# Normalization and projection in one stage, with the first weight blocks multiplied tile by tile

## What is computed

```python
for l in range(DEPTH):                                     # DEPTH = 2
    mix = token_mixer_block(x, w_in[l], ...)               # h = x @ w_in[l], four mixers, ... @ w_out[l]
    x = layer_norm(ALPHA * x + mix, ln1_g[l], ln1_b[l])
    ffn = peer_ffn(x, peer_wq[l], peer_keys[l], ...)       # q = x @ peer_wq[l], top-16 of 16384 experts, ...
    x = layer_norm(ALPHA * x + ffn, ln2_g[l], ln2_b[l])

def layer_norm(x, g, b):
    mu = jnp.mean(xf, -1, keepdims=True)
    var = jnp.mean(jnp.square(xf - mu), -1, keepdims=True)
    return (xf - mu) * lax.rsqrt(var + LN_EPS) * g + b
```

## Time and profile before

| | us |
|---|---|
| median of 3 runs | 4332.21 (4329.56 to 4340.54) |
| profiled execution, its own time | 4323.45 |
| its span, first to last instruction | 4321.9 |
| PE busy | 3888.1 (90%) |
| DVE busy | 2806.0 (65%) |
| ACT busy | 1492.0 (35%) |
| POOL busy | 1321.6 (31%) |
| DMA | 838 MB, 194 GB/s over the span |

### The profile page before, as it was taken

How to read it: one execution, slowest core, us unless ns; L and a number is a source line. 1 busy time by engine, 2 the same in 40 slices (tenths; PEclk the granted TensorE clock), 3 DMA queues, 4 the chain that set the end, 5 groups by cost and what they waited for, 6 DMA issues and landing times. The chain is left out here.

```text
span 4321.9 us, 55240 instructions
## 1 busy us (share of the span) xinstructions
PE 3888.1 (90%) x19266; PEld 3386.4 (78%) x19266; DVE 2806.0 (65%) x5410; ACT 1492.0 (35%) x2146; POOL 1321.6 (31%) x1141
## 2 busy tenths in 40 slices
PE   7987899799889999999679878987997899999995
PEld 6865687589779999988568666875997889999884
DVE  3254434379987888877622644343799888888775
ACT  2232322234563333333222323222345633333331
POOL 0010000046674655532000100000566745555320
PEclk9997899899999999999889878998999999999997
DMA  4210222334369999999332103223443699999993
GB/s 152 82 56 1 95 95 97 122 128 162 132 230 348 353 361 338 346 331 331 139 118 78 56 1 102 95 90 122 142 169 133 225 352 356 354 344 334 340 331 119
DMA packets 263691, 838.45 MB, mean 194 GB/s; under 512 B 19553, under 2 KB 68705, under 8 KB 238433
## 3 DMA queue, kind: packets, MB, share of 16 engines
q1 hardware_dynamic: 189792, 567.92, 36.8%
q0 software_dynamic: 73728, 268.47, 16.8%
HBM read 749.81 MB, written 86.51 MB: 194 GB/s over the span
## 5 line engine op out<-in xcount | busy, mean ns | idle before, releaser
L845 POOL TENSOR_TENSOR ahead_u_low<-u_raw,ahead_u_high 128x1024 fp32r<-128x1024 f32 x96 | 256.8, 2688 | 1304.3 <-ACT ahead_u_high L840 1304.0
L86 PE MATMUL bank<-v_low,w_high 128*128 128x512 f32 x1536 | 597.7, 389 | 0.0
L87 PE MATMUL bank<-v_high,w_high 128*128 128x512 f32 x1536 | 597.6, 389 | 0.0
L88 PE MATMUL bank<-v_high,w_low 128*128 128x512 f32 x1536 | 597.6, 389 | 0.0
L890 POOL DMA_INDIRECT far_rows<-peer_v_dram,far_index x256 | 372.9, 1457 | 500.4 <-DVE x_far L914 456.1
L890 POOL DMA_INDIRECT far_rows<-peer_u_rows_dram,far_index x256 | 370.1, 1446 | 352.7 <-DVE far_dots L896 302.6
L1524 DVE TENSOR_TENSOR v_low<-v_raw,v_high 128x1024 fp32r<-128x1024 f32 x256 | 301.8, 1221 | 230.5 <-ACT v_high L1469 230.5
L1469 ACT ACTIVATE v_high<-v_raw 128x1024 fp32r<-128x1024 f32 x256 | 257.1, 1052 | 498.2 <-PE bank L88 498.2
L86 PE MATMUL bank<-xT_low,u_high 128*128 128x384 f32 x1088 | 370.8, 341 | 31.8 <-DVE u_low L1505 26.1
L87 PE MATMUL bank<-xT_high,u_high 128*128 128x384 f32 x1088 | 369.8, 340 | 0.0
L88 PE MATMUL bank<-xT_high,u_low 128*128 128x384 f32 x1088 | 369.8, 340 | 0.0
(11 more groups left out here) (337 smaller groups left out, 8365.4 us busy)
## 6 DMA issues: line engine op xcount, KB each, us to landing
u_raw<-peer_u_dram SPq DMA_DIRECT2D x128, 1024.0 KB, 7.3
v_raw<-peer_v_dram SPq DMA_DIRECT2D x128, 1024.0 KB, 7.6
gates_scratch<-stage SPq DMA_DIRECT2D x12, 4096.0 KB, 13.8
G<-gates_scratch SPq DMA_DIRECT2D x64, 768.0 KB, 7.3
in_raw<-w_in_dram SPq DMA_DIRECT2D x40, 1024.0 KB, 5.3
mg_raw<-w_merge_dram SPq DMA_DIRECT2D x52, 768.0 KB, 4.2
hidden_scratch<-ahead_hid SPq DMA_DIRECT2D x60, 384.0 KB, 2.5
hid<-hidden_scratch SPq DMA_DIRECT2D x30, 768.0 KB, 6.7
```

The lines of the kernel that those rows point to most:

```text
L86: nc.tensor.matmul(out, lh, rl, start=first, stop=False)
L87: nc.tensor.matmul(out, lh, rh, start=False, stop=False)
L88: return nc.tensor.matmul(out, ll, rh, start=False, stop=last)
L845: eng.tensor_tensor(self.ul[:, c], self.ur[:, c], as_f32(self.uh[:, c]), ALU.subtract).then_inc(self.u_low, 1)
```

## The change

Every normalization is put into one stage with the projection that reads its result.

- `enter_stage` takes the place of the opening stage (layer 0) and of `norm_stage("ln2")` plus `project_stage("in")` (layer 1). SP asks for the first weight block before the tokens. Two token-major blocks come first and are multiplied tile by tile: PE runs `first(t, 0)` (24 matmuls), transposes tile t+1, runs `first(t, 1)` (24 matmuls). VectorE, per tile: normalize, in tiles 0 and 1 split a weight block, split the tile, and copy out the bank of the tile before, which waits for `first(t - 1, 1)`. ScalarE splits weight block 0 before its first square root. Constants are made behind this. The input goes no longer through the output tensor; layer 1 keeps its residual in `x_res`.
- `query_stage` takes the place of `norm_stage("ln1")` and `project_stage("pq")`. The first two blocks of `peer_wq` are multiplied in two halves of the tokens: 8 x 24 matmuls of 256 columns for tiles 0 and 1, as many for tiles 2 and 3. The first half stands among the transposes. Two `clear` calls come ahead of it, where there were none ahead of `norm_stage` and one ahead of `project_stage`.
- `final_stage` normalizes and stores the last output, without transposes; it asks for the two parameter rows first. The full `clear()` stands before it, and none behind it.
- In `spread_stage` the store of hidden values is issued ahead of the gates' store, no longer behind it.
- The layers are a Python loop: no branch back and constant addresses. `u_raw` lies in `merged`, the norm's buffers in `projT`, `far_rows` and `keys`.

The diff, cut to its core (removed functions are those printed above):

```diff
+            def normalize(self, dve, link, t, add, before=lambda half: None):
...
+                    part = tok[:, half * 512:(half + 1) * 512]
+                    before(half)
+                    if add:
+                        link(V.scalar_tensor_tensor(out=part, in0=part, scalar=ALPHA, in1=bank[2 * t + half][:],
+                                                    op0=ALU.mult, op1=ALU.add))
+                    link(V.bn_stats(self.stats[:, t % 2, half, :], part))
+                link(V.bn_aggr(self.mv[:, t, :], self.stats[:, t % 2, :, :]))
+                V.tensor_scalar(self.std[:, t:t + 1], self.mv[:, t, 1:2], LN_EPS, None, ALU.add).then_inc(s["var_ready"], 1)
+                dve.wait_ge(s["std_ready"], t + 1)
+                link(V.reciprocal(self.rstd[:, t:t + 1], self.std[:, t:t + 1]))
+                link(V.tensor_scalar(rt, tok, self.mv[:, t, 0:1], self.rstd[:, t:t + 1], ALU.subtract, ALU.mult))
+                if t == 0:
+                    dve.wait_ge(s["rows_in"], 32)
+                link(V.tensor_tensor(rt, rt, self.g_row, ALU.mult))
+                V.tensor_tensor(tok, rt, self.b_row, ALU.add).then_inc(s["x_ready"], 1)
...
+                        def load(j, b):
+                            for r in range(2):
+                                if 2 * j + b:
+                                    sp.wait_ge(w_low, 4 * j + 2 * b + r - 1)
+                                sp.dma_start(raw[:, r], a["w_in"][layer, block_of(j, b)][:, 4 * r:4 * r + 4, :]).then_inc(loaded[r], 16)
+                        def store(t):
+                            if layer:
+                                sp.wait_ge(s["x_ready"], t + 1)
+                                sp.dma_start(a["x_res"][:, t], norm.tokens(t)).then_inc(s["x_out"], 16)
+                        if layer:
+                            sp.dma_start(norm.g_row, a["ln2_g"][layer - 1].partition_broadcast(P)).then_inc(s["rows_in"], 16)
+                            sp.dma_start(norm.b_row, a["ln2_b"][layer - 1].partition_broadcast(P)).then_inc(s["rows_in"], 16)
+                            load(0, 0)
+                            for t in range(1, NT):
...
                             for t in range(NT):
...
+                                sp.dma_start(norm.tokens(t), a["x"].rearrange("o (t p) d -> p (o t) d", p=P)[:, t]).then_inc(x_in[t], 16)
+                                if t == 0:
+                                    load(0, 0)
+                            sp.dma_start(lbl[:], a["hgrn_lb_logits"]).then_inc(once["lb_in"], 16)
+                        load(0, 1)
+                        store(0)
+                        store(1)
+                        sp.dma_start(w_ff[:], a["w_ff"][layer]).then_inc(small_in, 16)
+                        for r in range(2):
+                            sp.wait_ge(w_low, 3 + r)
+                            sp.dma_start(raw[:, r], a["w_in"][layer, 0][:, 4 * r:4 * r + 4, :]).then_inc(loaded[r], 16)
+                        store(2)
+                        store(3)
+                        for r in range(2):
+                            sp.wait_ge(w_low, 5 + r)
+                            sp.dma_start(raw[:, r], a["w_in"][layer, 1][:, 4 * r:4 * r + 4, :]).then_inc(loaded[r], 16)
...
+                        def first(t, b):
+                            tok = slice(t * P, (t + 1) * P)
...
+                                if k % 4 == 0:
+                                    pe.wait_ge(s["low_done"], 2 * t + (2 if b else k // 4 + 1))
+                                    pe.wait_ge(w_low, 2 * b + k // 4 + 1)
+                                mm = matmul_split(nc, bank[2 * t + b][:], (xh[:, k, tok], xl[:, k, tok]), (wh[:, b, k, :], wl[:, b, k, :]),
+                                                  k == 0, k == KT - 1)
...
+                        turn(0)
+                        for t in range(NT):
+                            first(t, 0)
+                            if t + 1 < NT:
+                                turn(t + 1)
+                            first(t, 1)
+                        with pe.Fori(1, n_T + 1) as j:
+                            pair(j, False)
+                        pair(n_pairs - 1, True)
...
+                    def keep_first(eng, copy, parity, t):
+                        eng.wait_ge(mm_done, 2 * t + parity + 1)
+                        copy(projN[:, parity, t, :], bank[2 * t + parity][:]).then_inc(kept[parity], 1)
...
+                        def high(j, b):
+                            if isinstance(j, int) and j == 1:
+                                act.wait_ge(mm_done, 7 + b)
+                            elif not isinstance(j, int) or j:
+                                act.wait_ge(mm_done, 8 * j + 4 * b - 4)
+                            for r in range(2):
+                                act.wait_ge(loaded[r], 32 * j + 16 * b + 16)
+                                nc.scalar.activation(wh[:, b, 4 * r:4 * r + 4, :], raw[:, r], ACT.Copy).then_inc(w_high, 1)
+                        high(0, 0)
+                        for t in range(NT):
+                            if layer:
+                                norm.root(act, t)
+                            if t == 1:
+                                high(0, 1)
+                            norm.high(act, t)
+                            if t:
+                                keep_first(act, copy, 0, t - 1)
+                        high(1, 0)
+                        keep_first(act, copy, 0, NT - 1)
...
+                        for t in range(NT):
+                            if layer:
+                                if t:
+                                    dve.wait_ge(x_in[t], 16)
+                                norm.normalize(dve, link, t, add=t > 0)
+                            if t < 2:
+                                low(0, t)
+                            norm.low(dve, t)
+                            if t:
+                                keep_first(dve, copy, 1, t - 1)
+                        low(1, 0)
+                        keep_first(dve, copy, 1, NT - 1)
+                        low(1, 1)
+                        if layer == 0:
...
+        def query_stage(layer, merged, early, keys, mixed, qT, load_next):
...
+                        def load(n):
+                            for r in range(2):
+                                if n == 0:
+                                    sp.wait_ge(wo_low, 6 + 2 * r)
+                                else:
+                                    sp.wait_ge(w_low, 2 * n + r - 1)
+                                sp.dma_start(wq_raw[:, r], a["peer_wq"][layer, n][:, 4 * r:4 * r + 4, :]).then_inc(loaded[r], 16)
+                        def store(t):
+                            sp.wait_ge(s["x_ready"], t + 1)
+                            sp.dma_start(a["x_mid"][:, t - 1], norm.tokens(t)).then_inc(s["x_out"], 16)
...
+                        store(1)
+                        load(1)
+                        store(2)
+                        store(3)
+                        load(2)
+                        load(3)
+                        sp.wait_ge(s["x_out"], 16 * DT)
...
+                        def half_tokens(n, part):
+                            b, cols, tok = n // 4, slice(n % 4 * P, (n % 4 + 1) * P), slice(part * 2 * P, (part + 1) * 2 * P)
+                            pe.wait_ge(s["low_done"], 4 * part + 4 if part else max(4, n + 1))
+                            for k in range(KT):
+                                if n % 4 == 0 and k % 4 == 0 and part == 0:
+                                    pe.wait_ge(w_low, 2 * b + k // 4 + 1)
+                                mm = matmul_split(nc, bank[n][:, tok], (wq_h[:, b, k, cols], wq_l[:, b, k, cols]),
+                                                  (xh[:, k, tok], xl[:, k, tok]), k == 0, k == KT - 1)
+                            if part:
+                                mm.then_inc(mm_done, 1)
+                        out_projection(0, 2)
+                        out_projection(2, 1)
+                        turn(0)
+                        out_projection(3, 1)
+                        turn(1)
+                        for n in range(3):
+                            half_tokens(n, 0)
+                        turn(2)
+                        for n in range(3, 6):
+                            half_tokens(n, 0)
+                        turn(3)
+                        for n in range(6, 8):
+                            half_tokens(n, 0)
+                        for n in range(8):
+                            half_tokens(n, 1)
+                        for n in range(8):
+                            b, cols = n // 4, slice(n % 4 * P, (n % 4 + 1) * P)
+                            pe.wait_ge(kept[n % 2], n // 2 + 1)
+                            for k in range(KT):
+                                if n % 4 == 0 and k % 4 == 0:
+                                    pe.wait_ge(w_low, 4 + 2 * b + k // 4 + 1)
```

(28 more changed lines are left out.)

715 lines of the change are left out of this document (341 added, 374 removed).

## The result

| | before | after |
|---|---|---|
| median of the runs, us | 4332.8 (4329.56 to 4340.54) | 4256.09 (4245.99 to 4258.57) |
| span of the profiled execution | 4321.9 | 4244.3 |

What follows compares the result with a forecast made beforehand. PE was busy 3888 of 4321.9 us, so only its other 434 us, or what is shortened at either end, could move the time. Gains 9 + 23 + 32 + 10 + 0 = 74 us off 4332.2 gave 4258, range 4236 to 4298.

Steps and rivals of the forecast that it cites:

- The opening: Start of layer 0: weights asked for early, first real matmul at 14.7 instead of 29.9 us; gain 9 us.
- the rest at nothing: Rest of the kernel: constant addresses and no branch counted in the other sums, other load and store orders unchanged; 0 predicted.
- Between the layers: Experts' end to layer 1's input projection: tiles alternate with matmuls; gain 23 us, bounds 15 to 28.
- Rival (2): Between the layers the clock stays low in the alternation, 192 matmuls at 0.42 us; 4286 us, chance 0.12.
- Out-projection and query: Out-projection and query stages, both layers: matmuls on token halves overlap normalization; gain 32 us.
- The step with the widest bounds: Query halves: a 256-column matmul costs 0.125 us, giving 32 us for two layers; 42 at 0.112, -8 at 0.177.
- Rival (1): Query halves: a 256-column matmul costs as much as a 384-column one, 20 us lost per layer; 4298 us, chance 0.08.
- (6): Query halves: weight load stands in full ahead of each 256-column matmul, 36 us more per layer; 4330 us, chance 0.01.
- Rival (3): Query halves: clock stays low there too, 34 us more per layer; 4354 us with low clock between layers, chance 0.04.
- The end: Final normalization stage: shorter tiles, last tile neither transposed nor split, earlier loads, small clear gone; gain 10 us.
- Spread to experts: Spread's end: hidden values' store issued first starts experts 8.3 us earlier, but a later wait takes it back; gain 0.
- rival (4): Spread to experts: the reordered store's 16 us for both layers come through; 4242 us, chance 0.10.

Runs made afterwards that it cites:

- experiment 8: Changed kernel, but at the opening SP asks for all four token tiles before the first weight block; 4259.1 us, ratio to before 0.9834.
- Experiments 6 and 11: Changed kernel with each 256-column query matmul split: into two of 128 columns (6), 4353.6 us; into 192 and 64 columns (11), 4435.0 us.
- experiments 1 and 2: 1: changed kernel with the old order of the two spread stores put back, 4256.6 us; 2: kernel before with only that order turned round, 4335.5 us.

## Why the prediction was right

- **The opening**: 9.2 for 9, in part by luck. The start held, at 14.49 for 14.7, with the halves landed at 7.10 and 9.60 for 7.1 and 9.7, and experiment 8 confirms the price per MB. But the two rows that were named for it, 8.2 us for 2 MB and 5.3 for 1 MB, give 2.9 us per MB and 2.4 of latency, and not 2.5 and 2.3: the number was right and its working was not. And a tile's transposes among the matmuls cost 0.79 us (21.99 to 22.78), since they ran at the full clock, and not 1.7: 2.4 in all for 5.1. What took this back stands below, under the rest at nothing.
- **Between the layers**: 22.0 for 23. The start was 2.9 us too early in the forecast. The halves landed 8.6 and 11.1 us behind the stage's start for 6.9 and 9.4, and I left out a table load of 1.28 us ahead of the first root. On this the Trainium skill ("ScalarE: Activation LUTs", "What ACT_TABLE_LOAD costs") has 1.283 us for the load, and this trace agrees (1.28); it adds a drain of 1.38 for each switch, which no row here shows, the root starting at 2111.60, 0.02 behind the load. The alternation went as told, and with less of the clock: low until 2124.5 and once more for 3.4 us, so the charge of 5 us was too high: the 192 matmuls ended 80.7 us behind the stage's start, 76.8 without any charge, with 2.9 of the difference from the late start. Rival (2) is out by PEclk 0.94 from 2120 to 2182.
- **Out-projection and query**: 43 for 32, the largest miss, in the right direction and of 11 us. Per layer, the first query matmul came 2 us earlier behind the merge's end than forecast (64.9 for 66.9; the two clears cost 1.9 and 2.1 for 2.4), and the rest took 99.4 us for 102.7: 384 x 0.0045 = 1.7 because 256 columns take 0.1205 and not 0.125, the other 1.6 because the transposes of tiles 2 and 3 with the wait for tile 3's split took 2.8 for 4.0 and the wait for block 1 took 2.1 for 2.6. The clock was priced rightly: two low stretches of 3.4 us, half of which is 3.4, for 3.3 (1.8 in the first banks and 1.5). The step with the widest bounds, -8 to 42, was decided by reading 256 columns off the line through 384 and 512. Experiments 6 and 11 show that this was right with little to spare: the line ends between 192 and 256 columns, at a floor of 0.111. Nothing on record had told where it ends, so that it held at 256 is luck in part. The bound from the 128-column row, 0.112, was the floor itself and no part of a line. Rival (1) is out, and so is (6): load and columns do not add up even at 64 columns.
- **Rival (3)**, the low clock in the halves, did not come, but my reason against it, that matmuls standing back to back run at 2.4 GHz, is refuted by experiments 6 and 11. It held at 256 columns and failed for 34 us at 128. A chance of 0.04 was too little for what was then known. Nor does the trace of before bear out what the prediction cites on transposes and the clock. The 0.50 of rows 3 stands over a stretch in which PE was idle for 21 of 29 us and so does not tell. At the opening PE did nothing but the 32 transposes from 8.99 on (rows 4), and the clock rose among them, at 12.57: the first sixteen starts stand 0.213 us apart, the last fourteen 0.109. Its window:

  ```profile
  12.60:14.40 1.80, 1.80 (x17) 1.57 (x15) 1.80 (x4) 1.73 (x4) 0.00 (x0) 1.00 1.02 410
  ```

- **The end**: 9.2 for 10, with the parameter rows landing ahead of the tokens and a tile's period of 7.01 for 6.93.
- **Spread to experts**: -2.3 for 0, and rival (4) is out by experiments 1 and 2. The reason given (u(1) is asked for only behind the gates' store) is right for half of it: with the request moved, 4 us of each layer's 8 come back, and the other half hangs on the gates' own load and the products behind it, which I had not named.
- **The rest at nothing**: the six channel-major blocks of the input projection, which the change only puts behind two token-major ones, got slower. Their matmuls stand 0.2333 us apart at the full clock, before 0.2289, in both layers: 576 x 0.0044 = 2.5 us a layer. In the opening this made good the transposes that had been priced too high, and between the layers it took back what the clock had left. The mixer and merge stages lost 1.4 and 1.7 us. It is hardly an accident: these two took 437.2 to 437.8 us in the two kernels with the loop (each layer on its own), and 438.7 to 441.7 in the twelve written out but for one layer of one, 436.9. About 1 us of it lies in a stretch with long idle times of PE (365 to 415 us before, 356 to 407 after), where the granted clock was 0.70 and is 0.67. Why stays open for both; no experiment was made on them.
- The sum was 74 of 77.6 us. The errors of +11, -3.1, -2.3 and four of 1 or less partly cancel, and inside the opening and the stretch between the layers larger ones do. The count of the chances had 0.94, 0.02 and 0.04 where the rivals' own add up to 0.95, 0.01 and 0.04.

## What to carry to other kernels

Between a normalization and its projection, it is the interleaving of tiles with multiplications that paid here, and an engine's order paid again: look for what stands in an in-order engine behind an operation that waits for a transfer, such as a root of 0.2 us behind a split. Cut matmuls for the sake of overlap only down to a width at which columns still set the time and the clock still comes up; here 256 columns gave 18 us over whole tokens, 128 lost 84, and 192 with 64 lost 166. And an empty stretch that a change only moves is still worth a look: clearing semaphores while others worked gave 18 us, a quarter of what the whole change had given. And compare the stages that a change leaves alone: a matmul slower by 0.0044 us cost 5 us here.

## What the runs showed of the hardware

- Matmuls that each load 128 columns of weights never stood closer than a floor, by the medians: 0.111 to 0.112 us for 64, 128 and 192 columns at 2.4 GHz, 0.213 at 1.2 GHz, there for 256 columns too. At 2.4 GHz 256 columns took 0.120, 384 took 0.173 to 0.178, and 512 took 0.227 (experts) to 0.234 (projections).
- The granted clock can be low, and fall, with no idle time of PE: matmuls of 128 columns back to back ran at 1.2 GHz for 33.7 us and then at 2.4 GHz, and of 192 and 64 columns at 1.2 GHz for 61 us and more, where 256-column ones reached 2.4 GHz after 3.4 us. The Trainium skill ("TensorE: Matmul & The Clock Gate", "HAM oscillation — how this bites in real kernels") tells of the clock falling where PE waits between bursts; the stops of the query stage agree (3.4 us low behind 4.95 and 2.10 us of idle time), while one of the two stops of 2.2 us between the layers was followed by no fall, and these two kernels had the first stop alone and stayed or fell low behind it.
- The clock rose with nothing but transposes on PE, at the opening of the kernel before: 32 back to back, 0.213 us apart up to 12.57 us and 0.109 behind it.
- Clearing 155 semaphores takes GpSimd 65 ns each and holds all engines for 10.8 us with its barriers, in each of the two places where it stands.
- SP stands in the issue of a transfer behind the 4 MB store, for 8.16 us with the store just issued; two issues of 1 MB each, 5.4 us later, took it 4.94 us where they take 1.40 with the store landed. The store took 14.9 us there and 14.2 in the changed kernel.
